# State-space output map: powers 5 to 8 made from powers 1 to 4, and whole-row transfers into the chunk map

## The reference, cut to what matters

```python
mod = c_act @ w_ada[i] + b_ada[i]
h = modulate(rms_norm(x, norm_g[i, 0]), sh1, sc1)
# s5_mixer, per group g: complex state h, input map bb, output map c, decay a
h_t = a * h_(t-1) + bb @ u_t
y_t = Re(c @ h_t) + d * u_t
z = gelu(y); gl = z @ w_glu
h = gl[..., :1024] * sigmoid(gl[..., 1024:])
```

## Time and profile before

| | us |
|---|---|
| median of 3 runs (1131.28 to 1132.77) | 1132.59 |
| the profiled execution's own time | 1132.53 |
| its span | 1130.4 |
| outside the span | 2.1 |
| PE busy | 1000.4 |
| DVE busy | 824.1 |
| ACT busy | 621.4 |

### The profile page before, as it was taken

One profiled execution on the slowest core, in us unless ns is written; L12 is line 12 of the kernel. 1 busy time (PEld: TensorE's weight loads), 2 busy tenths in 40 slices (PEclk: granted clock), 3 DMA queues, 4 the chain that ended last, 5 costly groups with the idle time before them and its releaser, 6 DMA issues.

```text
span 1130.4 us, 17539 instructions
## 1 busy us (share of the span) xinstructions
PE 1000.4 (88%) x6586; PEld 826.4 (73%) x6587; DVE 824.1 (73%) x1116; ACT 621.4 (55%) x764; POOL 29.5 (3%) x73
## 2 busy tenths in 40 slices
PE   0775787999999987779879999999999999999993
PEld 0553476888989877556667888888888888888882
DVE  7899885345353547568366888898988888898884
ACT  4421265333343445456346776867777686867762
POOL 3000000000000000000100000000000000000000
PEclk9978789899999997879959999999999999999998
DMA  9847993296878675240427999999999999999951
GB/s 258 334 158 231 258 340 135 97 355 227 297 245 308 245 287 227 77 149 1 132 74 250 363 333 352 320 351 331 335 342 332 348 322 350 323 348 338 333 206 57
DMA packets 199107, 292.95 MB, mean 259 GB/s; under 512 B 18293, under 2 KB 164970, under 8 KB 198778
## 3 DMA queue, kind: packets, MB, share of 16 engines
q1 hardware_dynamic: 189114, 283.32, 72.6%
q10 hardware_dynamic: 8160, 5.85, 1.9%
q0 software_dynamic: 1760, 2.78, 1.0%
HBM read 287.39 MB, written 2.11 MB: 256 GB/s over the span
## 4 chain that ended last, share of the span: by engine, by line
issue 52%; PE 30%; DVE 9%; DMA 3%; ACT 2%; SPq 2%; POOL 0%; DVEq 0%; ACTq 0%; POOLq 0%
PE ps L588 8%; PE ps L589 7%; PE ps L590 7%; PE ps L632 2%; DMA raw<-in_w_ada 1%; SPq L408 1%; DMA raw<-in_ffn_w_in 1%; DMA mod_rows<-ada_wide 1%; PE ps L946 1%; PE ps L937 1%; ACT w_hi L1159 1%; PE ps L738 1%; PE ps L929 1%; PE ps L920 1%; PE ps L729 0%
## 5 line engine op out<-in xcount | busy, mean ns | idle before, releaser
L2035 DVE TENSOR_TENSOR w_lo<-raw,w_hi 128x2048 fp32r<-128x2048 f32 x162 | 366.0, 2287 | 64.8 <-ACT w_hi L1439 64.8
L1439 ACT ACTIVATE w_hi<-raw 128x2048 fp32r<-128x2048 f32 x162 | 303.9, 1909 | 0.0
L1522 DVE TENSOR_TENSOR w_lo<-raw,w_hi 128x2048 fp32r<-128x2048 f32 (+3 forms) x59 | 131.6, 2249 | 112.7 <-ACT w_hi L1159 111.3
L588 PE MATMUL ps<-w_hi,xe_hi 128*128 128x512 f32 x448 | 179.3, 400 | 1.3 <-DVE xe_lo L2012 1.3
L590 PE MATMUL ps<-w_hi,xe_lo 128*128 128x512 f32 x448 | 175.4, 392 | 0.0
L589 PE MATMUL ps<-w_lo,xe_hi 128*128 128x512 f32 x448 | 174.8, 390 | 0.0
L1159 ACT ACTIVATE w_hi<-raw 128x2048 fp32r<-128x2048 f32 (+3 forms) x59 | 109.3, 1879 | 97.1 <-DMA raw<-in_ffn_w_in 80.7
L588 PE MATMUL ps<-act_hi,w_hi 128*128 128x256 f32 x352 | 102.6, 292 | 1.2 <-DVE act_lo L1690 0.8
L589 PE MATMUL ps<-act_lo,w_hi 128*128 128x256 f32 x352 | 100.3, 285 | 0.0
L590 PE MATMUL ps<-act_hi,w_lo 128*128 128x256 f32 x352 | 100.3, 285 | 0.0
L590 PEld LDWEIGHTS ps<-w_hi,xe_lo 128*128 128x128 f32 x448 | 84.1, 188 | 17.8
(11 more groups left out here) (392 smaller groups left out, 1586.1 us busy)
## 6 DMA issues: line engine op xcount, KB each, us to landing
raw<-in_moe_w_in SPq DMA_DIRECT2D x224, 512.0 KB, 5.2
raw<-in_moe_w_out SPq DMA_DIRECT2D x56, 1024.0 KB, 7.0
raw<-in_w_ada SPq DMA_DIRECT2D x48, 1024.0 KB, 9.4
raw<-in_ffn_w_in SPq DMA_DIRECT2D x44, 512.0 KB, 7.9
raw<-in_ffn_w_out SPq DMA_DIRECT2D x11, 1024.0 KB, 11.4
raw<-in_ssm_w_glu SPq DMA_DIRECT2D x16, 512.0 KB, 8.0
raw<-in_mla_w_o SPq DMA_DIRECT2D x4, 1024.0 KB, 8.3
raw<-in_mla_w_uq SPq DMA_DIRECT2D x3, 768.0 KB, 6.9
```

Of the source, the lines that this page charges most:

```text
L588: mm(dst, st[0], mv[0], start=first, stop=False)
L1439: af(HI[:, (V_MOE + m) % RING, :], RAW[:, (RAW_OF_W[V_MOE] + m) % RING, :], cp).then_inc(hi_done, 1)
L1522: tt_(LO[:, slot, 0:w], RAW[:, RAW_OF_W[v] % RING, 0:w], HI[:, slot, 0:w].bitcast(F32), ALU.subtract)\
L2035: tt_(LO[:, slot, :], RAW[:, (RAW_OF_W[V_MOE] + m) % RING, :], HI[:, slot, :].bitcast(F32), ALU.subtract)\
```

## The change

`O` has its powers 1 to 4 made as before, in four parts of eight group pairs (`o_base`, six instructions of 512 elements). Powers 5 to 8 are those times `a^4`, a complex number per partition and group pair: ScalarE multiplies the low powers, with real and imaginary part exchanged, by the imaginary part of `a^4` into a new tile s_low_turned (16 instructions of 64 elements a part), and VectorE multiplies by the real part and adds (`o_high`, 8 instructions of 128 elements a part). Power 0 is a copy of `c` on ScalarE. The new tile lies on the end of the state input map, so ScalarE waits until `state_inputs` is done (`v_ps`).

`M` and the strips get another layout, in which the rows of a block transfer are contiguous (16 rows of up to 1024 elements in place of 16 x 8 pieces of up to 128). SyncE issues the first half's transfers before its wait of load 21 and the second half's at load 26 in place of 24. On TensorE `outputs(0)` is split, and its first part comes before `ada(20..23)`.

```diff
-        M = at("s5_chunk_map", [P, NG, P], 64)
+        M = at("s5_chunk_map", [P, 2, 4, L, 8, GH], 64)
         S = at("s5_state", [P, 2, GI, NJ], 104)
+        TD = at("s5_low_turned", [P, 2, 8, 2, 4 * GH], 104)
...
             for i in rows:
                 for c4 in range(4):
                     p0 = 32 * c4 + GH * (c4 % 2)
-                    eng.dma_start(M[GH * i:GH * (i + 1), 32 * part + c4:32 * part + 32:4, GH * i:P],
-                                  STRIPS[part][p0:p0 + GH, :, :, 0:(L - i) * GH].rearrange("p x b n -> p (x b) n")).then_inc(m_in[part], 16)
+                    eng.dma_start(M[GH * i:GH * (i + 1), part, c4, i:L, :, :],
+                                  STRIPS[part][p0:p0 + GH, 0:L - i, :, :]).then_inc(m_in[part], 16)
...
             for r, (kind, n) in enumerate(STREAM[:RAW_OF_W[V_MOE + looped]]):
+                if r in (RING + 15, RING + 20):
+                    m_blocks(sp, (r - RING - 15) // 5, range(0, L, 2))
                 if r >= RING:
...
-                if r in (RING + 15, RING + 18):
-                    m_blocks(sp, (r - RING - 15) // 3, range(0, L, 2))
...
-                pe.wait_ge(o_ok, (4, 8)[part])
+                pe.wait_ge(o_ok, (2, 4)[part])
+                pe.wait_ge(o_zero, 2)
...
             strips(1)
+            output_inputs(0)
             for n in range(20, 24):
                 ada(n)
-            outputs(0)
-            outputs(1)
+            output_states(0)
+            output_inputs(1)
+            output_states(1)
...
-            wide(2)
-            wide(3)
+            act.wait_ge(v_ps, 2)
+            for j in range(4):
+                act.wait_ge(o_low, 2 * j + 2)
+                if j >= 2:
+                    act.wait_ge(o_ok, j - 1)
+                for k in range(8):
+                    gi = 8 * j + k
+                    for c in range(2):
+                        last = af(TD[:, j % 2, k, c, :], O[:, 1 - c, gi, 1:5, :].rearrange("p t h -> p (t h)"), cp,
+                                  scale=PW[:, 1, gi, 4:5] if c == 0 else PW[:, 0, gi, 8:9])
+                last.then_inc(o_turn, 1)
+                if j == 0:
+                    af(O[:, 0, :, 0, :], CT[:, 0, :, :], cp).then_inc(o_zero, 1)
+                    af(O[:, 1, :, 0, :], CT[:, 1, :, :], cp, scale=-1.0).then_inc(o_zero, 1)
+                if j == 1:
+                    wide(2)
+                if j == 2:
+                    wide(3)
             strip_copies(0)
...
+            def o_high(j):
+
+                dve.wait_ge(o_turn, j + 1)
+                dve.wait_ge(o_low, 2 * j + 2)
+                for k in range(8):
+                    gi = 8 * j + k
+                    last = stt(out=O[:, :, gi, 5:9, :].rearrange("p c t h -> p c (t h)"),
+                               in0=O[:, :, gi, 1:5, :].rearrange("p c t h -> p c (t h)"), scalar=PW[:, 0, gi, 4:5],
+                               in1=TD[:, j % 2, k, :, :], op0=ALU.mult, op1=ALU.add)
+                last.then_inc(o_ok, 1)
...
-            for n, q in enumerate([*range(GI // 4), None]):
-                o_part(q).then_inc(o_ok, 1)
-                dve.wait_ge(o_ok, n + 1)
-                if n == 4:
+            for j in range(4):
+                o_base(j)
+                if j:
+                    o_high(j - 1)
+                if j == 2:
                     mod_rows(2)
-                    mod_rows(3)
-                if n == 5:
-                    mod_columns(3)
+            mod_rows(3)
+            o_high(3)
+            mod_columns(3)
+            dve.wait_ge(o_ok, 4)
```

More of the change, by code:

```diff
@@ L396, in moe_loop, with chunk_map @@
             pair(NE // 2 - 1, False, True)
-        def map_slot(g):
-            return g // GI * 16 + g // 16 % 2 * GI + g % 16
+        def chunk_map(g):
+            gi = g % GI
+            return M[:, gi // 16, gi % 4, :, g // GI * 4 + gi % 16 // 4, :]
         def m_blocks(eng, part, rows):
@@ L721, in y_tile, with output_inputs @@
                 return cols.rearrange("p (t a h) -> p a t h", t=L, a=2)[:, gg % 2, :, :]
-            def outputs(hf):
+            def output_inputs(hf):
                 pe.wait_ge(s_ok, 2 * hf + 1)
@@ L728, in outputs @@
                     for c4 in range(4):
-                        mm(PS[32 * c4:32 * c4 + 32, q, :].rearrange("p (a n) -> p a n", a=16), M[96:P, 0, 0:32],
-                           M[96:P, 0:16, 0:32], start=True, stop=False)
+                        mm(PS[32 * c4:32 * c4 + 32, q, :], M[96:P, 0, 0, 0, 0:2, :].rearrange("p x h -> p (x h)"),
+                           M[96:P, 0, 0, 0:4, :, :].rearrange("p t x h -> p (t x h)"), start=True, stop=False)
                 pe.wait_ge(m_in[hf], 16 * 32)
-                dts = (2 * hf, 2 * hf + 1)
-                for dt in dts:
+                for dt in (2 * hf, 2 * hf + 1):
                     for a in range(2):
@@ L737, in outputs, with output_states @@
                                 g = 8 * (dt + 4 * g2) + 2 * c4 + a
-                                last = mm(y_tile(g), U[:, g, :], M[:, map_slot(g), :].rearrange("p (t h) -> p t h", t=L),
+                                last = mm(y_tile(g), U[:, g, :], chunk_map(g),
                                           start=False, stop=False)
                 last.then_inc(y_ps, 1)
+            def output_states(hf):
                 pe.wait_ge(s_ok, 2 * hf + 2)
-                for dt in dts:
+                for dt in (2 * hf, 2 * hf + 1):
                     for a in range(2):
@@ L1229, in strip_copies @@
                 if part:
-                    act.wait_ge(o_ok, 9)
+                    act.wait_ge(o_ok, 4)
                 for g2 in range(2):
-                    af(STRIPS[part][:, g2, :, :].rearrange("p a n -> p (a n)"), PS[:, 6 + g2, :], cp).then_inc(strip_ok, 1)
+                    af(STRIPS[part][:, :, 4 * g2:4 * g2 + 4, :].rearrange("p t q h -> p q t h"),
+                       PS[:, 6 + g2, :].rearrange("p (q t h) -> p q t h", q=4, t=L), cp).then_inc(strip_ok, 1)
             def gelus(n):
@@ L1612, in _ @@
                 last = v_.tensor_copy(PWR[:, :, :, t], PW[:, 0:2, :, L - 1 - t])
+            ts_(PW[:, 0, :, 8], PW[:, 1, :, 4], -1.0, None, ALU.mult)
             link_(last)
@@ L1700, in o_part @@
                 dst = [O[:, c, g, lags, :] for c in range(2)]
-                t0, t1 = [RTMP[:, c, :].rearrange("p (g t h) -> p g t h", g=sh[1], t=sh[2]) for c in range(2)]
+                t0, t1 = [RTMP[:, c, :].rearrange("p (g t h) -> p g t h", g=8, t=4) for c in range(2)]
                 tt_(dst[0], cr, pr, ALU.mult)
@@ L1705, in o_part @@
                 link_(tt_(t1, cr, pi, ALU.mult))
-                tt_(dst[0], dst[0], t0, ALU.subtract)
-                return stt(out=dst[1], in0=dst[1], scalar=-1.0, in1=t1, op0=ALU.mult, op1=ALU.subtract)
+                tt_(dst[0], dst[0], t0, ALU.subtract).then_inc(o_low, 1)
+                stt(out=dst[1], in0=dst[1], scalar=-1.0, in1=t1, op0=ALU.mult, op1=ALU.subtract).then_inc(o_low, 1)
+            def o_high(j):
[7 more added lines that the diff above has]
+                last.then_inc(o_ok, 1)
             r_block(0)
```

15 lines of the change are left out of this document (8 added, 7 removed).

## The result

The changed kernel is slower: 1144.62 us as the median of four runs (1141.46 to 1146.67) against 1132.26 for the kernel before on the same chip, ratio 1.012 with a 95% interval of 1.009 to 1.015. My forecast was 1132.8, with 1127.8 to 1137.6 as its range. The profiled execution of after took 1146.67 us, its span 1144.6 (before: 1132.53 and 1130.4); it is the slowest of the four, 2 us above their median. One execution of e1 (2036 us) and one of the kernel before (2546 us), with a granted clock of 1.00 where all others show 0.93 to 0.95, are left out of every figure. `w_glu` starts at 159.24, where before it started at 145.89: 13.35 us later; from there to the span's end it is 985.4 against 984.5 us. The loss was made ahead of `w_glu`.

What follows compares the result with a forecast made beforehand. The bound was taken to be the chain from first strip copy through SyncE's 16 block issues to weight loads 21 to 23, not VectorE. 13.2 - 5.2 - 0.7 - 7.0 = +0.3 us on 1132.53 gave 1132.8, range 1127.8 to 1137.6.

Steps and rivals of the forecast that it cites:

- What bounds it: Before `w_glu`: strip copy, SyncE's 16 block issues, then loads 21 to 23 bound it; VectorE has 4 to 5 us spare.
- Pace of VectorE and ScalarE: In map building: VectorE's high parts 2.2 us each, ScalarE's small products 0.24 us apart, 3.84 us for 16.
- Term 1: ScalarE's first strip copy comes later, behind 64 small products: +13.2 us, bounds +9.5 to +17.5.
- Term 2: SyncE's 16 first-half block transfers issue in 0.42 us each, not 0.75: -5.2 us, bounds -6.8 to 0.
- Term 3: Weight loads 21 to 23 take 12.2 us from first issue to last landing, not 12.94: -0.7 us, bounds -1.9 and 0.
- Term 4: TensorE's zeroing and first input products run before loads 21 to 23 land, hidden with 6 us of cover: -7.0 us.
- What stands behind: After the last modulation product: second-half blocks land at 131 to 132, mostly covered by TensorE's 1.95 us pause; nothing added.
- a change of the pauses: Sign of a wrong prediction: TensorE's pauses at the end of the outputs go away or grow.
- The slower rival: Block issues stay dear as SyncE's and ScalarE's queues take turns, 0.60 us a step: 1135 to 1139 us, chance 0.30.
- Its further part: Second-half blocks, behind 5 MB of loads in one queue, land as late as 135.5, 2.4 us past TensorE's pause.
- The faster ones: Shorter block issues, quicker loads and row, shorter pauses: -4 to -5 us, 1128; all faster cases together chance 0.30.
- VectorE as the bound: VectorE's map building decides, so 3 us or all 10.7 come off: 1129.5 us, chance 0.03, counted as faster.

Runs made afterwards that it cites:

- e1: The changed kernel with SyncE issuing the second half's 16 block transfers ahead of the first `w_glu` load, as the kernel before does; 1140.2 us, ratio 1.0083.
- e3: The kernel before with the shared powers alone, keeping the old block form and the old SyncE and TensorE order; 1143.5 us, ratio 1.0125.
- e7: The changed kernel with SyncE's second-half blocks ahead of the `w_glu` loads and the first strip copied before ScalarE's fourth 16 products; 1132.1 us, ratio 1.0017.
- e2: The kernel before with the whole-row form of strips and chunk map alone; 1129.6 us, ratio 0.9996.
- x2: The changed kernel with as many block transfers but only the first half of every row, so its output is wrong; 1139.8 us, ratio 1.0077.
- b1: The kernel before with SyncE issuing the second half's block transfers behind the first two `w_glu` loads; 1134.3 us, ratio 1.0028.
- e8: The changed kernel with SyncE's second-half blocks ahead of the `w_glu` loads, the first strip copied early and TensorE's old order; 1139.0 us, ratio 1.0065.
- e5: The changed kernel with TensorE's old order, zeroing and first input products behind modulation products 20 to 23; 1141.0 us, ratio 1.0106.
- p1: The kernel before with row blocks 6 and 7 of each half, a quarter of the block transfers, on GpSimd's queue; 1126.1 us, ratio 0.9954.
- p2: The changed kernel with SyncE's second-half blocks ahead of the `w_glu` loads, the first strip copied early and a quarter of the blocks on GpSimd; 1129.0 us, ratio 0.9990.
- x1: The changed kernel with a quarter of the block transfers carrying the same bytes, so three quarters of the chunk map are wrong; 1144.6 us, ratio 1.0127.
- e4: The changed kernel with ScalarE's two copies of the first strip ahead of its fourth 16 small products; 1135.2 us, ratio 1.0048.

## Why the prediction was wrong

**What bounds it.** Right up to the modulation loads. The chain still goes through the strip copy and SyncE's first 16 issues, and VectorE's scan was 4.4 us earlier and TensorE never waited for it. But the chain no longer ends in a load: from SyncE's load issues it goes on through the `w_glu` issues and the second half's 16 to the landing of the last block at 145.73.

**Pace of VectorE and ScalarE.** Right: high parts 2.19 us for 8 (0.27 each), ScalarE's products 3.93 us for 16 (0.245), the first at 82.94 (83.0 forecast), VectorE idle 4.26 us before its first high part (before `mod_rows` it was 0.84, not 2, since the row came sooner).

**Term 1, the late first strip.** +13.2 forecast, 105.37 - 93.83 = +11.5 measured; the row's transfer took 3.72 us, not 5.0. Nearly right in size, and e3 shows that alone it moves `w_glu` by 11.6. The mechanism was half of it. I had written that the first strips, "ready near 97, are not what it waits for". They were ready at 98.6, and e7 shows that 5.9 of the 11.5 us are left when the copies run as soon as the strip is there.

**Term 2, the transfers.** The first step that failed: -5.2 forecast, 11.95 down to 11.60 us, -0.35 measured. I had priced an issue by other transfers ("Nearest: one of 8 rows issues in 0.28 us, one of 128 in 0.35"), although 0.60 stood there as the least of 16 between the same two tiles. e2 and x2 show that neither the number of pieces nor the bytes set it.

**Term 3, loads 21 to 23.** -0.7 forecast; 131.84 - 116.97 = 14.9 us against 12.94, +1.9 measured, outside its bounds. The cause stays open. What stands close behind the loads does not explain it: in e3 the second half's blocks begin 2.0 us behind the first load's issue (before: 6.5), in b1 two more loads stand directly behind, and their loads take 12.5 and 12.1 us. The form of the blocks is a suspect that I had not named: with the old form the profiles show 12.1 to 12.9 us (before, b1, e3), with whole rows 13.6 (e2, x2) to 18.8 (e8). Only e2 changes the form alone, and there it is 0.6 us.

**Term 4, the moved products.** Forecast -7.0 and hidden with 6 us of cover. They ran at 122.69, not before 120, but ahead of the load at 131.84, and the state products began right behind it. The saving was made. e5 shows it hidden again by what comes later, e7 against e8 shows it at 5.4 us or more.

Up to here the terms as measured give 11.5 - 0.35 + 1.9 - 7.0 = +6.0 us, and the state products did start at 132.84 against 126.82: +6.0.

**What stands behind.** The second step that failed, and the dearest: the second half's blocks were forecast to land at 131 to 132, covered by TensorE's pause; they were there at 145.73. That is the other 13.35 - 6.0 = 7.3 us. I had let SyncE issue ahead while loads travel, and counted only the loads' 2.6 us each. The pause of 1.95 us, which I had kept in place as cover, is gone: the wait stands where it stood, and one of my signs of being wrong, a change of the pauses, came with it. In the trace the third and fourth `w_glu` issue last 4.2 us each, so SyncE reaches the blocks at 129.05, needs 14.3 us for the 16 where I had none on the path, and 2.95 to land. e1 shows 5.3 us of the 7.3 to be the place in the queue.

**The slower rival.** I gave it 0.30 and 1135 to 1139. Its price of an issue, 0.60, came out; its reason did not. SyncE's issues from 132.47 to 142.78 take 0.59 us as a rule, and ScalarE issued in that time only one row's transfer, so nothing took turns with them. The rule of the Trainium skill (Perfetto Trace Analysis, DMA Instruction, HWDGE) that the shown time includes a wait for a shared generator is not what made these issues dear: alone and together they cost the same. Its further part, the late second half, was the right step at a third of its size (2.4 us of 7.3), since I priced loads and not issues.

**The faster ones, and VectorE as the bound.** None came. That VectorE was not the bound is shown from the other side by p1, in which it becomes it.

The parts by `w_glu`'s start in the profiles: shared powers +11.6 (e3), then row form and TensorE's order -3.5 (e3 to e1), then the second half's blocks moved in SyncE's queue +5.3 (e1 to after). The sum is 13.4, as it must be in a row of differences. Each is one profile per kernel, and two profiles of the same stage differ by 2 to 3 us before the edit bites (ScalarE's first product at 80.20 in e4, 82.94 in after), so the parts are good to about that.

## What to carry to other kernels

When work moves from a busy engine to an idle one, look at what the idle one does next on the critical chain: here 64 small products, 16 us on an engine that had time, cost the kernel 11.6 us, half because the first strip's own products waited for them and half because two copies stood behind them. A transfer's issue is work on a queue: count the issues ahead of a critical transfer at the price of the same kind of transfer, and do not put large loads in front of it (two of them cost 5.3 us in the changed kernel and 2.4 in the one before). And before giving an engine relief, make it the bound: p1, which only spread issues over a third queue, won 0.46%, where the change lost 1.2%. Even then the relief must not delay what comes first, as p2 shows.

## What the runs showed of the hardware

- An issue of a transfer from one tile into another took 0.59 to 0.61 us on SyncE and 0.61 to 0.66 on ScalarE (medians of 16) for 8 to 64 KB, in 128 pieces or 16 rows, on SyncE the same with ScalarE's queue busy or quiet. GpSimd issued such blocks in 4.25 / 8 = 0.53 us each (p1), while SyncE issued its own.
- The Trainium skill (DMA: Bandwidth & Descriptors, Issuing engines are not separate DMA queues) says that starting transfers from several engines saves only the sequencer's time, usually small beside the transfer. Here that time was on the chain: p1, which does nothing but spread issues, gained 0.46%.
- An issue can last several us. Behind three loads of 1 MB and two of 512 KB issued within 4 us, the next two of 512 KB took 4.26 and 4.19 us, and the block behind them 3.37; in b1 the same two took 3.61 and 3.67. In x1 128 KB behind 448 KB took 4.25. That a queue takes only so much at a time and holds the next issue until some of it has landed would fit all of these; no run varies it alone.
- ScalarE's queue issued transfers between the instructions of a batch that stands ahead of them in the program, the first 1.14 us behind the batch's first product in e7 (1.13 in e4), though the strip was there 2 us earlier in e7.
- The granted clock was 0.50 (1.2 GHz) when `w_glu` began, in both kernels, after TensorE had stood idle. Its products lasted 0.43 us until 165.12 in after, 5.9 us from the start, and until 150.50 in before, 4.6 us: by my estimate 0.6 us (half of the 1.3 us more at half the clock) of the 0.9 by which the rest was longer.
- TensorE's pauses that wait for nothing shown (1.95 and 2.15 us in before) moved from 0.6 to 3.8 us between kernels, and hid in a wait where there was one: after has a single one of 0.63. Their share in small differences is not separated: e2's two are 1.3 us longer than those of before, and in p1 waits for VectorE stand in their place.
